# Six experts instead of five in fixed places of a mixture-of-experts order, with one more expert loaded early

## The reference

```python
x = x + g1 * y                                    # attention
h = rms_norm(x, norm2_g[l]) * (1.0 + sc2) + sh2
x = x + g2 * moe_ffn(h, w_router, router_bias, w_gate_up, w_down, shared_gate_up, shared_down)

# moe_ffn
scores = sigmoid(xf @ w_router)                   # 256 x 64
idx    = the 6 experts of a token (by groups of 8 experts)
routed = for each token the sum over its 6 experts of  weight * swiglu(x, w_gu[e], w_dn[e])
swiglu = (silu(x @ g) * (x @ u)) @ w_dn           # w_gu: 1024 x 512, w_dn: 256 x 1024 per expert
```

## Time and profile before

| | |
|---|---|
| median of 3 runs | 1265.64 us (1265.19 to 1266.31) |
| the profiled execution, first to last instruction (its span) | 1263.2 us |
| what lies around the span, median less span | 2.4 us |
| TensorE matmuls | 1089.7 us busy, 86% of the span |
| VectorE | 505.3 us, 40% |
| ScalarE | 248.6 us, 20% |
| DMA | 502.24 MB, mean 398 GB/s |
| mean granted TensorE clock | 0.950 |

### The profile page before, as it was taken

How to read it: one execution, slowest core, us unless ns; L and a number is a source line. 1 busy time by engine, 2 the same in 40 slices (tenths; PEclk the granted TensorE clock), 3 DMA queues, 4 the chain that set the end, 5 groups by cost and what they waited for, 6 DMA issues and landing times.

```text
span 1263.2 us, 17095 instructions
## 1 busy us (share of the span) xinstructions
PE 1089.7 (86%) x6524; PEld 597.4 (47%) x6524; DVE 505.3 (40%) x1131; ACT 248.6 (20%) x575; POOL 0.4 (0%) x5
## 2 busy tenths in 40 slices
PE   7999999997887878687869999999788797878785
PEld 6887586543333424243326678655333242434332
DVE  3697975334123122212226887533312222312231
ACT  1021722211001111111113472221101111101110
POOL 0000000000000000000000000000000000000000
PEclk9999999999889899999989999999988998989998
DMA  9999999999999999999999927899999999999996
GB/s 346 392 409 414 407 360 362 414 423 422 424 423 423 423 424 422 424 424 424 422 416 392 406 104 276 355 411 423 422 424 424 423 423 424 423 423 424 424 424 279
DMA packets 99289, 502.24 MB, mean 398 GB/s; under 512 B 10985, under 2 KB 35462, under 8 KB 44934
## 3 DMA queue, kind: packets, MB, share of 16 engines
q1 hardware_dynamic: 98742, 500.92, 97.1%
q10 hardware_dynamic: 464, 0.20, 0.1%
HBM read 500.04 MB, written 1.05 MB: 397 GB/s over the span
## 4 chain that ended last, share of the span: by engine, by line
SPq 49%; PE 31%; DMA 9%; DVE 5%; issue 4%; ACT 0%; DVEq 0%
SPq L595 44%; PE bank L779 25%; DMA ring<-in_moe_w_gate_up 4%; SPq L704 3%; PE bank L782 2%; DMA ring<-in_ada_w 2%; DMA w_gu_x<-in_ada_w 2%; DMA ring<-in_moe_w_down 1%; SPq L602 1%; PE bank L906 1%; PE bank L1055 1%; DVE s_sb L1809 1%; PE bank L1264 1%; PE bank L978 1%; DVE s_sb L1803 1%
## 5 line engine op out<-in xcount | busy, mean ns | idle before, releaser
L779 PE MATMUL bank<-w_gu,ring 128*32 128x512 f32 (+1 forms) x1120 | 294.9, 703 | 107.3 <-DMA w_gu<-in_moe_w_gate_up 34.1
L779 PEld LDWEIGHTS bank<-w_gu,ring 128*32 128x32 f32 (+1 forms) x1120 | 77.5, 133 | 273.5 <-issue 273.0
L1963 DVE TENSOR_TENSOR hh<-sg,bank 128x256 f32<-128x256 f32 x44 | 27.3, 621 | 399.2 <-ACT sg L1549 399.2
L779 PE MATMUL bank<-ring 128*32 128x512 f32 (+1 forms) x336 | 169.7, 654 | 10.2 <-DMA gate<-in_moe_w_gate_up 7.8
L779 PE MATMUL bank<-w_gu,hhT 128*32 128x512 f32 (+1 forms) x416 | 138.4, 596 | 7.3 <-DMA ring<-in_moe_w_down 4.9
L779 PE MATMUL bank<-w_dn,ring 128*32 128x512 f32 x240 | 130.1, 792 | 16.5 <-DMA w_dn<-in_moe_w_gate_up 8.2
L779 PE MATMUL bank<-w_gu_x,ring 128*32 128x512 f32 (+1 forms) x272 | 127.0, 669 | 5.5 <-DMA ring<-in_moe_w_gate_up 5.5
L1549 ACT ACTIVATE sg<-bank 128x256 f32<-128x256 f32 x44 | 16.9, 384 | 480.5 <-PE bank L779 480.5
L1980 DVE SCALAR_TENSOR_TENSOR bank<-bank,w_slot,gate 128x512 f32<-128x512 f32 x88 | 66.6, 759 | 97.3 <-PE bank L779 97.2
L779 PE MATMUL bank<-sel,h_hi 128*128 128x256 f32 x352 | 87.8, 290 | 0.0
L1429 ACT ACTIVATE y_hi<-bank 128x512 fp32r<-128x512 f32 x88 | 52.6, 597 | 162.0 <-DVE bank L1980 161.8
(11 more groups left out here) (317 smaller groups left out, 1706.4 us busy)
## 6 DMA issues: line engine op xcount, KB each, us to landing
w_gu<-in_moe_w_gate_up SPq DMA_DIRECT2D x130, 1024.0 KB, 25.5
w_gu<-in_moe_w_down SPq DMA_DIRECT2D x46, 1024.0 KB, 26.4
ring<-in_moe_w_gate_up SPq DMA_DIRECT2D x42, 1024.0 KB, 26.2
ring<-in_ada_w SPq DMA_DIRECT2D x36, 1024.0 KB, 11.6
w_gu_x<-in_moe_w_gate_up SPq DMA_DIRECT2D x30, 1024.0 KB, 26.0
w_dn<-in_moe_w_gate_up SPq DMA_DIRECT2D x28, 1024.0 KB, 26.3
w_gu_x<-in_moe_w_down SPq DMA_DIRECT2D x14, 1024.0 KB, 26.4
w_dn<-in_moe_w_down SPq DMA_DIRECT2D x14, 1024.0 KB, 26.0
```

The source lines that it names most:

```text
L779: return nc.tensor.matmul(o, a, b, start=first, stop=last)
L1963: v.tensor_tensor(hh[:, :].rearrange("s (f p) -> s p f", f=FE // P), sg[:, :].rearrange("s (p f) -> s p f", f=FE // P), bank[b][:, FE:2 * ...
```

## The change

`FIXED` becomes 6. The sixth expert (number 5) gets a pass of its own kind, the fourth, with two narrow ones; the later pass of that kind ("m") is taken out and its wide expert goes into an ordinary pair. The largest expert's 96 slots belong to rank 6 now. There are still 22 passes, 23 experts of 64 or more slots and 41 of 32.

The sixth's two gate-up halves join the pieces that are loaded before the wait for the order, into unit 13 (a ring slot) and unit 17 (the router's place). Both units were before in the list of those free for the first loads after the order. Its down piece is assigned like the others.

```diff
-FIXED = 5
+FIXED = 6
-LAST_WIDE = FIXED + 17
+LAST_WIDE = FIXED + 16
     add_pass((4, 64), (next(narrow), 32), (next(narrow), 32))
-    for kind in "qqpqpqpqpxqpqpmpqpq":
+    add_pass((5, 64), (next(narrow), 32), (next(narrow), 32))
+    for kind in "qqpqpqpqpxqpqppqpq":
...
-LAST_UNITS = ((("dn", 3, 0), 12), (("dn", 4, 0), 14))
+SIXTH = RANK_OF.index(5)
+LAST_UNITS = ((("dn", 3, 0), 12), (("gu", SIXTH, 0), 13), (("gu", SIXTH, 1), 17), (("dn", 4, 0), 14))
...
-    free = [(turn_read(item), u) for item, u in unit.items() if u != ROWS_UNIT] + [(turn_of["shared_up"], 15), (turn_of["shared_up"], 16),
-                                                                                   (-1, ROUTER_UNIT), (-1, RING_UNIT)]
+    free = [(turn_read(item), u) for item, u in unit.items() if u != ROWS_UNIT] + [(turn_of["shared_up"], 15), (turn_of["shared_up"], 16)]
...
+            ring_last.append([c[0] for i, c in enumerate(chunks[:number[("sgu", l, 0)]]) if ring_of(i) == free[0]][-1])
...
+                elif u == RING_UNIT:
+                    freed(sp, ring_last[l])
                 elif u == ROUTER_UNIT:
                     sp.wait_ge(sem("logits"), l + 1)
...
             def fixed_loads(l, items):
                 for item, _ in items:
-                    unit_load(l, item, item[1])
+                    unit_load(l, item, RANK_OF[item[1]])
```

More of the change, by code:

```diff
@@ L85, in plan_passes @@
             add_pass(*[(next(wide), 64) for _ in range(2)])
-        elif kind == "m":
-            add_pass((next(wide), 64), (next(narrow), 32), (next(narrow), 32))
         else:
@@ L457, in ring_of @@
             return (i + 4) % RING
-        unit_at, xg = [], []
+        unit_at, xg, ring_last = [], [], []
         for l in range(2):
```

## The result

The changed kernel takes 1269.62 us (median of 6 runs, 1268.42 to 1270.88), the kernel before on the same chip 1265.26 us (median of five, 1264.75 to 1266.31). A sixth run of the kernel before took 6024.46 us and is left out; with it the median would be 1265.45 us. The ratio is 1.0034, 95% interval [1.0022, 1.0046]: 4.4 us slower. A second set of runs gave 1268.7 us, ratio 1.003 [1.0018, 1.0042]. The forecast was 1266.4 us, with a range to 1268.9; of the three terms of its sum the third, the stop of SyncE between the layers, had the right sign and not the right size.

What follows compares the result with a forecast made beforehand. Expert phases were taken as bound by weight transfer, with TensorE pacing their openings. Span 1263.2 us -0.3 (layer 0) -0.2 (layer 1) +1.3 (between layers) gave 1264.0, plus 2.4 to the median: 1266.4 us, range 1263.6 to 1268.9.

Steps and rivals of the forecast that it cites:

- the three terms of its sum: Against the span of 1263.2 us: -0.3 in layer 0, -0.2 in layer 1, +1.3 between the layers.
- the stop of SyncE: End of layer 0: SyncE waits about 15 us for the last down product before the second modulation block; cost 1.3 us.
- The holes: DMA shortfalls at 202-211 and 799-809 us: two early loads nearly fill each, but the 9.7 us is given back at once.
- The first rival: Holes at both phase openings are filled and the time stays won: 1257.2 us, chance 0.07.
- The -0.5 us that I counted: Gain in both layers' openings from the load after the first 13 no longer queueing behind others: 0.3 and 0.2 us.
- The moved pass: Pass of one wide and two narrow experts, now fourth, nine loads instead of twelve: counted at 0.
- My upper end: Between the layers: second modulation block lands in 5.9 us, third 3.2 us later, at 666.2 us, 3.0 us late.
- The slack of 0.2 us: Start of layer 1: the third modulation block could land 0.2 us later without delay, since `xn` is ready about 664.6 us.
- the signs that I had named: Forecast wrong if load after the 13th leaves well before 240.8, DMA falls short 290-640, or third block lands by 663.3/after 666 us.
- The lower bound of the range: Whole kernel: 1263.6 us, from the free-wait case less the larger opening gain and 0.6 us of run scatter.
- The second: Rival: SyncE's stop between the layers costs its upper end, 3.0 us, and the openings win nothing: 1268.6 us, chance 0.14.
- The third: Rival: SyncE's wait between the layers is free, third modulation block at 663.2 us: 1265.1 us, chance 0.17, counted as no change.

Runs made afterwards that it cites:

- e1: Changed kernel with two pieces of the last pass exchanged between units 13 and 17, so the second modulation block avoids the last down product; 1266.01 us, ratio 1.0007.
- e3: Changed kernel with only the new pass order: the sixth expert's gate-up halves load behind the order wait again, units 13 and 17 free; 1265.01 us, ratio 1.0001.
- e2: Kernel before plus one wait: SyncE waits for the last down product before issuing layer 1's second modulation block; 1268.41 us, ratio 1.0028.
- e5: Changed kernel with unused matmuls on constants ahead of TensorE's waits for the second and third modulation blocks; 1268.41 us, ratio 1.0024.
- e6: Changed kernel with TensorE's matmuls on the third modulation block moved behind layer 1's transposes; 1268.17 us, ratio 1.0022.
- e7: Kernel before with the first load behind the order held, in each layer, until TensorE has done the first half of pass 0; 1270.88 us, ratio 1.0044.
- the second trace: Trace of the unmodified changed kernel run again beside the kernel before; median 1268.7 us, ratio 1.003, profiled execution 1270.87 us.

## Why the prediction was wrong, point by point

**The holes.** Right: 360 and 350 GB/s where there were 201 and 202, and the load behind the 13th leaves with the same half of pass 2. The first rival (1257.2 us) is refuted by e1, which has the filled holes without the stop and is not faster. The -0.5 us that I counted was wrong, though: in layer 0 that load landed 4.9 to 7.4 us after its issue in the five traces with filled holes, where I had 5.3. I took "nearly empty queue" for "lands faster". e1 measures the two moved loads at +1.0 us against e3, barely more than can be told.

**The moved pass.** Right at 0, as far as e3 can tell.

**The stop of SyncE.** This is the step that failed: "So the second block lands at 657.1 + 5.0 = 662.1 us, and the third 2.48 us later, at 664.6 instead of 663.2: 1.4 us." The mechanism, the place and the order of events were right: the wait of 15 to 17 us at L721, the second block issued when the last down product is done, all of layer 1 late by the third block. The term was mis-sized: 3.2 us instead of 1.3 by e2, which adds this wait alone, 2.7 us by the changed kernel less e1, which is without it, and 3.0 to 5.2 us between the marks of the five traces. Its parts:

- From the issue of the second block to the landing of the third I had 5.0 + 2.48 = 7.5 us. Measured were 8.0, 9.4, 8.1, 9.3 and 9.5 us. The landing of the second block was 4.8, 6.8, 4.7, 6.4 and 6.9 us after its issue, that of the third 2.5 to 3.4 us behind it. My upper end, 5.9 + 3.2, would have been the better value; I took "the rows of the same tensor", the median of five of the earlier trace rows, as the price of one on the critical path. The five are not alike: 4.9, 4.8, 8.1, 5.0 and 7.1 us, since the third and the fifth were issued 0.4 us behind another, as the third block is behind the second. From the issue of the first of such a pair to the landing of the other it was 8.5 and 7.5 us, so the trace before held the price of the pair. The lines below are the first pair, issued at 758.77 and 759.14 us. The Trainium skill (DMA: Bandwidth & Descriptors, Bandwidth) lists 6.15 us for 1 MB. Both this and the formula by which I had estimated 4.4 are given there for transfers issued from GpSimd, and these are SyncE's; the traces, 4.7 to 6.9 us, lie on both sides of the 6.15 and above the formula.

```profile
ring<-in_ada_w SPq DMA_DIRECT2D x1, 1024.0 KB, 4.8
ring<-in_ada_w SPq DMA_DIRECT2D x1, 1024.0 KB, 8.1
```

- In the first trace of the changed kernel SyncE was released at 658.6 us instead of 657.1. There the last down product itself ran slowly (1.07 us for a matmul that takes 0.62 in the other traces), after TensorE had waited 2.42 us for its weights, and the stop hands this on; before and in e1 the same wait is 2.49 us and no fall follows. The landing was fast in that execution, and the sum came out near that of e5 and e6 by chance.
- What a lower clock costs I had put at nothing without a reason: up to 2.0 us when the wait for a block is followed by 0.50.

The slack of 0.2 us was not there. e7, e1, e3 and the kernel before have 12.0 us between the marks with a third block 7.5 to 8.2 us behind the last load, so an earlier block wins nothing; but the first trace of the changed kernel and e5 have it 3.3 and 3.1 us later behind that load than before, and the projections by exactly as much.

Of the signs that I had named, "if the third block lands by 663.3 us or after 666 us" came true. The lower bound of the range doesn't come out of its own terms either: 1265.1 less 0.6 us of gain and 0.6 us of scatter is 1263.9, not 1263.6 us. It decides nothing here.

**Rivals.** The second (slower, 1268.6 us, chance 0.14) is what happened, with its own point of decision, a third block after 666.2 us: it landed at 666.57 us in one trace and, right at that point, at 666.17 in the other. Its mechanism, both landings at their longest, is that of the second trace, of e5 and of e6; the first trace passed the point by its slow down product. I gave it 0.14 because I took the shorter row for each of two landings; the longer row of each was as good a guess, and both came due together. The third (the wait is free) is refuted by e2.

**The sum as measured**: the stop +3.2 us (e2), the moved loads +1.0 us (e1 against e3), the passes 0: 4.2 us, and the changed kernel is 3.5 to 4.4 us slower. No version tried beats the kernel before; e3 equals it.

## What to carry over

- A hole in a transfer queue is worth filling only if places come free sooner as well. Count the loads up to the next instruction that waits for a place: if the count is the same with and without the early loads, the gain is given back there.
- When units are assigned by a rule, look at who reads a unit last before a phase ends. A load that waits for the very last product stops all loads behind it in the queue's program order; an exchange of two units in the last pass takes 2.7 us of the loss back.
- Price a load on the critical path in an empty queue by the longest landing seen, not by the median, and loads issued behind each other as a group. Count a stretch of TensorE at half its clock behind a long wait as possible, and not as sure.

## What the runs showed of the hardware

A load of 1 MiB issued into an all but empty queue landed after 4.7 and 4.8 us in two executions and after 6.4 to 6.9 us in three, with nearly the same work ahead of it. In the second trace of the changed kernel (6.8 us) the queue moved less in that landing although four more loads had been issued behind the second block, from 661 to 663 us (e2 has 422 GB/s in the same stretch):

```profile
661.00:663.00 2.00, 0.33 (x4) 0.00 (x0) 0.97 (x3) 1.78 (x7) 0.00 (x0) 1.00 0.76 262
```

What makes the difference stays open; no run told it apart. Between the end of the last gate-up products and the projections, waits of TensorE of 2.1 to 2.5 us came with a granted clock of 0.50 in four places (the down product of the first trace, the second block in the second, the third block in e2, the transposes behind the second block in e6), and with none in five others (the third block in the first trace, and the down product before, in e1, in the second trace and in e5). Whether it comes at such a wait thus can't be said from its length alone; with waits under 1 us ahead of the blocks in e5 it did not come.
